# A trunk step on one core: the sample tokens in quarters of the columns, and the first loads and statistics in another order

## What is computed

```
x   = layernorm(x; ln_in)                      # every token over its 1024 columns
h, states = mixer(x)                           # one in-projection, mLSTM and HGRN2 heads, one out-projection
x1  = layernorm(ALPHA * x + h; ln1)
logits = x1 @ w_router + b_router              # 32 experts
top_v, top_i = top_k(logits, 4); gates = softmax(top_v)
y   = sum over the 4 picked experts of gate * expert(x1)   # clamped SwiGLU, 1024 -> 1024 -> 1024
y  += sigmoid(x1 @ w_ple_gate) * (p @ w_ple_proj)
out = layernorm(ALPHA * x1 + y; ln2)
```

## Time and profile before

| | before |
|---|---|
| median of 3 runs | 1262.06 us (1261.76 to 1264.11) |
| the profiled execution, its own time | 1263.85 us |
| its span in the profile | 1262.0 us |
| PE busy | 1166.6 us (92%) |
| DVE busy | 400.7 us (32%) |
| ACT busy | 178.2 us (14%) |
| DMA | 441.92 MB, mean 350 GB/s |

### The profile page before, as it was taken

The page is one execution under the profiler, slowest core; times in us unless marked ns, Lnnn a source line. Parts: engine busy times, 40 slices in busy tenths (PEclk is TensorE's granted clock), DMA queues, the critical chain, the costliest instruction groups (busy, mean ns, idle before and its releaser), DMA issues.

```text
span 1262.0 us, 13214 instructions
## 1 busy us (share of the span) xinstructions
PE 1166.6 (92%) x5599; PEld 483.0 (38%) x5599; DVE 400.7 (32%) x643; ACT 178.2 (14%) x321; POOL 77.2 (6%) x77
## 2 busy tenths in 40 slices
PE   3999999799999997899999999999999999998984
PEld 2777774643333332242333333332323232322221
DVE  6866423841223130112322222232323222214115
ACT  1253242411010110020101010100101010110001
POOL 3100141400101030000000000000000000000000
PEclk9999999899999998999999999999999999999987
DMA  9562111579999999999999999999999999999891
GB/s 313 176 180 67 67 68 67 208 300 420 421 421 421 422 420 386 421 422 421 416 422 421 421 421 421 406 422 420 421 420 421 420 422 412 422 421 413 370 420 55
DMA packets 70029, 441.92 MB, mean 350 GB/s; under 512 B 7824, under 2 KB 7856, under 8 KB 20816
## 3 DMA queue, kind: packets, MB, share of 16 engines
q1 hardware_dynamic: 65168, 425.52, 82.6%
q0 software_dynamic: 4800, 15.51, 3.7%
HBM read 436.28 MB, written 4.73 MB: 349 GB/s over the span
## 4 chain that ended last, share of the span: by engine, by line
PE 70%; DMA 19%; DVE 8%; ACT 2%; issue 1%; SPq 1%; DVEq 0%
PE ps L935 41%; DMA more<-in_w_up 11%; PE ps L543 9%; PE ps L919 5%; PE ps L871 3%; DVE y_s L1740 2%; PE ps L761 2%; DMA ring<-in_w_gate 2%; DMA more<-in_w_down 2%; DMA more<-in_w_gate 2%; PE ps L926 1%; PE ps L571 1%; DVE h_s L1738 1%; ACT hTe L1084 1%; DMA ring<-in_w_up 1%; PE ps L951 1%
## 5 line engine op out<-in xcount | busy, mean ns | idle before, releaser
L935 PE MATMUL ps<-ring,xTe 128*64 128x512 f32 x1536 | 357.4, 602 | 13.4 <-DMA ring<-in_w_up 9.1
L935 PEld LDWEIGHTS ps<-ring,xTe 128*64 128x64 f32 x1536 | 103.9, 136 | 242.0 <-issue 241.8
L1722 DVE TENSOR_TENSOR xs<-xs,ps 128x512 f32<-128x512 f32 (+1 forms) x128 | 70.5, 551 | 365.3 <-PE ps L919 364.7
L935 PE MATMUL ps<-ring,hTe 128*64 128x512 f32 x768 | 181.4, 613 | 4.5 <-DMA ring<-in_w_down 4.5
L935 PE MATMUL ps<-more,xTe 128*64 128x512 f32 x512 | 117.1, 598 | 6.0 <-DMA more<-in_w_up 5.8
L543 PE MATMUL ps<-xT,ring 128*128 128x288 f32 x448 | 116.6, 417 | 1.0 <-PE ps L543 0.6
L935 PEld LDWEIGHTS ps<-ring,hTe 128*64 128x64 f32 x768 | 51.7, 139 | 119.7 <-issue 119.4
L543 PEld LDWEIGHTS ps<-xT,ring 128*128 128x128 f32 x448 | 85.8, 196 | 25.6 <-issue 2.3
L919 PE MATMUL ps<-y_s,GT 128*128 128x512 f32 (+1 forms) x256 | 81.8, 518 | 1.2 <-ACT y_s L1084 1.2
L1738 DVE TENSOR_SCALAR h_s<-ps 128x512 f32<-128x512 f32 x32 | 21.8, 681 | 159.3 <-PE ps L935 159.3
L1754 DVE TENSOR_TENSOR ple<-ple,ps 128x512 f32<-128x512 f32 (+1 forms) x64 | 35.3, 551 | 105.0 <-PE ps L871 90.8
(11 more groups left out here) (344 smaller groups left out, 796.2 us busy)
## 6 DMA issues: line engine op xcount, KB each, us to landing
ring<-in_w_gate SPq DMA_DIRECT2D x96, 1024.0 KB, 10.7
ring<-in_w_up SPq DMA_DIRECT2D x96, 1024.0 KB, 12.1
ring<-in_w_down SPq DMA_DIRECT2D x96, 1024.0 KB, 13.6
more<-in_w_gate SPq DMA_DIRECT2D x32, 1024.0 KB, 12.2
more<-in_w_up SPq DMA_DIRECT2D x32, 1024.0 KB, 12.1
more<-in_w_down SPq DMA_DIRECT2D x32, 1024.0 KB, 13.8
ring<-in_w_in SPq DMA_DIRECT2D x28, 512.0 KB, 6.1
ring<-in_w_out SPq DMA_DIRECT2D x8, 512.0 KB, 5.0
```

Source lines behind the costliest of these rows:

```text
L935: last = mm(ps[64 * q:64 * q + 64, bank0 + half, :], lhs(k, q), wide(t)[:, k % 2, half * 512:(half + 1) * 512], start=False, stop=k == KT - 1)
L1722: last = tt(xs[0:r, i, c], xs[0:r, i, c], new, ALU.add)
```

## The change

1. **Sample tokens in quarters.** The residual of the 32 sample tokens is now `xq`, 128 partitions x 256 columns: partitions 32q to 32q+31 hold columns 256q to 256q+255. Every operation on it is one of 128 x 256 in place of four of 32 x 256 or one of 32 x 1024. Its vectors are `ln_q` (quarters too; eight small loads for each norm). Its statistics need a sum over the four quarters: DVE writes `lnq` (`spread_stats`), PE multiplies it with a matrix of ones and zeros (`row_stats`), and `bn_aggr` reads 24 numbers from PSUM. Two transposes of 128 x 128 in place of eight of 32 x 128 give `xT`; for the router ACT writes each token four times (`xT4`), so that logits and choices lie on all 128 partitions, and the two copies of `row_of` go. The bf16 parts of the samples are made on DVE and ACT in `xbq`, and PE (`sample_rows`) and ACT (`copy_sample_rows`) bring them to `xb_s`. POOL has the subtractions of the prompt tiles only.
2. **The start.** All of x is loaded first, then a quarter of the constants, the vectors, the first four ring slots, the rest of the constants, the other slots. POOL begins its loads when all of x is there. DVE makes the statistics of the three tiles first, then waits for all ten vector loads (L1462 of the new code) and applies the three norms.
3. **Routing stage.** `x1` is now written without a stride; `part` and `rest` of the prompt tiles work with the stride instead. PE routes all three tiles, counts ranks in two steps, and does both `prompt_states` after `sample_ranks`. `OH` is written in halves; the first gather waits for the first half. `neg_v`, a copy for the states and the copy of the counts come after it.
4. **End.** DVE makes the statistics of each tile right after its last share is added. The result of the samples leaves in four loads.

The diff, cut to its core:

```
@@ sync
-            for i, (_, r) in enumerate(TILES):
-                sp.dma_start(xs[0:r, i, :], x_src[i]).then_inc(S[f"x_in{i}"], 16)
-                if i == 0:
-                    sp.dma_start(ln_g[:, :], a["ln_in_g"].partition_broadcast(P)).then_inc(S["ln1_in"], 16)
-                    sp.dma_start(ln_b[:, :], a["ln_in_b"].partition_broadcast(P)).then_inc(S["ln1_in"], 16)
-                    sp.dma_start(cf[:, :], a["const_f"]).then_inc(S["const_in"], 16)
+            for i in range(2):
+                sp.dma_start(xs[:, i, :], x_src[i]).then_inc(S[f"x_in{i}"], 16)
+            for q, x in enumerate(quarters(x_src[2])):
+                sp.dma_start(xq[q * NS:(q + 1) * NS, :], x).then_inc(S["x_in2"], 16)
+            sp.dma_start(cf[:, 0:CF_FIRST], a["const_f"][:, 0:CF_FIRST]).then_inc(S["ident_in"], 16)
+            for n, v in enumerate(("ln_in_g", "ln_in_b")):
+                sp.dma_start((ln_g, ln_b)[n][:, :], a[v].partition_broadcast(P)).then_inc(S["ln1_in"], 16)
+                for q in range(4):
+                    sp.dma_start(ln_q[q * NS:(q + 1) * NS, n, :],
+                                 a[v][q * QW:(q + 1) * QW].partition_broadcast(NS)).then_inc(S["ln1_in"], 16)
...
-            for c0 in W_GROUPS:
+            for n, c0 in enumerate(W_GROUPS):
+                if n == 1:
+                    sp.dma_start(cf[:, CF_FIRST:], a["const_f"][:, CF_FIRST:]).then_inc(S["const_in"], 16)
@@ gpsimd
+            pool.wait_ge(S["x_in2"], 64)
...
-            for i in range(3):
+                out = rests[:, i, :]
+                nc.gpsimd.tensor_tensor(natural(out), natural(out if q else x1[:, i, :]), by_row(xb[:, i, q, :]),
+                                        ALU.subtract).then_inc(S["rest_ok"], 1)
+
+            for i in range(2):
                 for q in range(2):
                     rest(i, q)
@@ tensor
+            def row_stats(n):
+                pe.wait_ge(S["lnq_ok"], n)
+                mm(ps[:, STAT_BANK, 0:24], cf[:, CF_SAME:CF_SAME + P], lnq[:, :, :].rearrange("p q s -> p (q s)"),
+                   start=True, stop=True).then_inc(S["lnq_mm"], 1)
...
-            route(0)
             transpose_normed(1)
+            row_stats(2)
+            route(0)
+            transpose_normed(2)
             route(1)
+            route(2)
+            prompt_ranks()
+            sample_rows()
+            sample_ranks()
             prompt_states_b()
-            transpose_normed(2)
-            route(2)
...
-            pe.wait_ge(S["xT_ok"], 12)
-            prompt_states_a()
-            ranks()
-            pe.wait_ge(S["part_ok"], 9)
-            pe.wait_ge(S["OH_ok"], 1)
+            prompt_states_a()
...
+            pe.wait_ge(S["part_ok"], 8)
+            pe.wait_ge(S["OH_first"], 1)
@@ scalar
+                if i < 2:
+                    f(by_row(xb[:, i, q, :]), natural(rests[:, i, :] if q else x1[:, i, :]), ACT.Copy).then_inc(S["part_ok"], 1)
+                else:
+                    f(xbq[:, q, :], rest_q[:, :] if q else x1q[:, :], ACT.Copy).then_inc(S["partq_ok"], 1)
...
+            part(2, 0)
+            copy_xT(2, 6, 0)
             part(1, 1)
-            part(2, 0)
-            part(1, 2)
-            copy_xT(2, 6, 0)
             part(2, 1)
             part(2, 2)
+            part(1, 2)
+            copy_sample_rows()
@@ vector
+            def spread_stats():
+                tt(lnq[:, :, :], lns[:, 2, 0:1, :].to_broadcast([P, 4, 6]),
+                   cf[:, CF_QUARTER:CF_QUARTER + 4].unsqueeze(2).to_broadcast([P, 4, 6]), ALU.mult).then_inc(S["lnq_ok"], 1)
...
             for i in range(3):
-                dve.wait_ge(S[f"x_in{i}"], 16)
+                dve.wait_ge(S[f"x_in{i}"], 16 if i < 2 else 64)
+                tile_stats(i)
+                if i == 2:
+                    dve.wait_ge(S["ident_in"], 16)
+                    spread_stats()
                 norm_stats(i, i + 1)
-                if i == 0:
-                    dve.wait_ge(S["ln1_in"], 32)
+            dve.wait_ge(S["ln1_in"], 160)
+            for i in range(3):
                 norm_apply(i, i + 1)
...
+            def rest_of_samples(q):
+                dve.wait_ge(S["partq_ok"], q + 1)
+                tt(rest_q[:, :], rest_q[:, :] if q else x1q[:, :], xbq[:, q, :], ALU.subtract).then_inc(S["restq_ok"], 1)
+
+            select(0)
+            rest_of_samples(0)
+            select(1)
+            rest_of_samples(1)
+            select(2)
...
-            for q in (1, 2):
-                step(nc.vector.tensor_copy(row_of[q * NS:(q + 1) * NS, 2, :], row_of[0:NS, 2, :]))
-            step(nc.vector.tensor_copy(ex[:, 3, :], ps[:, 4, P + 3 * NE:P + 4 * NE]))
...
-            add_shares(NPAIR - 1)
+            add_shares(NPAIR - 1, tile_stats)
```

More of the change, by code:

```diff
@@ L103, in trunk_step, with quarters @@
     x_src = [a["x_prompt"][0, 0:P, :], a["x_prompt"][0, P:NP, :], a["x_sample"].rearrange("b t d -> (b t) d")]
+    def quarters(rows):
+        return [rows[:, q * QW:(q + 1) * QW] for q in range(4)]
     p_src = [a["p_prompt"][0, 0, 0:P, :], a["p_prompt"][0, 0, P:NP, :],
@@ L1334, in _, with tile_stats @@
             nc.vector.memset(eps[:, 2:3], 1.0).then_inc(S["setup"], 1)
+            def tile_stats(i, done=None):
+                x = tokens(i)
+                for q in range(2 if i < 2 else 1):
+                    last = nc.vector.bn_stats(lns[:, i, q, :], x[:, q * 512:(q + 1) * 512] if i < 2 else x)
+                    (done or step)(last)
+            def spread_stats():
+                tt(lnq[:, :, :], lns[:, 2, 0:1, :].to_broadcast([P, 4, 6]),
+                   cf[:, CF_QUARTER:CF_QUARTER + 4].unsqueeze(2).to_broadcast([P, 4, 6]), ALU.mult).then_inc(S["lnq_ok"], 1)
@@ L1336, in norm_stats @@
             def norm_stats(i, n):
-                r = TILES[i][1]
-                x = xs[0:r, i, :]
-                for q in range(2):
-                    step(nc.vector.bn_stats(lns[0:r, i, q, :], x[:, q * 512:(q + 1) * 512]))
+                if i == 2:
+                    dve.wait_ge(S["lnq_mm"], n // 3)
                 if n > 3:
                     dve.wait_ge(S["ln_std"], n - 3)
-                nc.vector.bn_aggr(mv[0:r, i, 0:2], lns[0:r, i, :, :].rearrange("p q s -> p (q s)")).then_inc(S["ln_var"], 1)
+                stats = lns[:, i, :, :].rearrange("p q s -> p (q s)") if i < 2 else ps[:, STAT_BANK, 0:24]
@@ L1346, in norm_apply @@
+                nc.vector.bn_aggr(mv[:, i, 0:2], stats).then_inc(S["ln_var"], 1)
             def norm_apply(i, n):
-                r = TILES[i][1]
-                x = xs[0:r, i, :]
+                x = tokens(i)
                 dve.wait_ge(S["ln_var"], n)
-                g, b = (ln_g, ln_b) if n < 7 else (ln2_g, ln2_b)
-                step(stt(x, x, mv[0:r, i, 0:1], g[0:r, :], ALU.subtract, ALU.mult))
-                dve.wait_ge(S["ln_std"], n)
-                step(nc.vector.reciprocal(mv[0:r, i, 3:4], mv[0:r, i, 2:3]))
```

250 lines of the change are left out of this document (155 added, 95 removed).

## The result

| | before | changed |
|---|---|---|
| median | 1261.93 us (4 runs, 1261.76 to 1264.11) | **1276.54 us** (4 runs, 1275.21 to 1277.31) |
| span of the profiled execution | 1262.0 us | 1274.5 us |
| first product of pair 0 | 256.70 | 268.06 |
| last copy of `y_s` | 1239.27 | 1252.85 |
| ACT busy | 178.2 us | 201.4 us |

The ratio (changed over before) is 1.0111, with a 95% interval of 1.0093 to 1.0128: slower by 14.6 us, where 7.7 us less were forecast. The span grew by 12.5 us: start and mixer -2.9 (up to the out-projection's long run of products, at 204.77 in place of 207.68), from there to the first product of pair 0 +14.3, expert stage +2.2, end -1.1. The profile's chain shows what came onto the path: ACT has 4% of it where it had 2, and POOL a first 1%.

What follows compares the result with a forecast made beforehand. The expert stage was taken as DMA-bound and fixed in length, shifting with pair 0's first product. -2.8 (start) - 3.5 (routing) + 0.6 (experts) - 2.0 (end) = -7.7 from the 1262.06 us median gives 1254.3 us; range 1248 to 1260.

Steps and rivals of the forecast that it cites:

- I take 1.0: Routing stage: ACT's and POOL's strided split of the prompt tiles costs 1.0 times the plain one; other bound 1.6.
- The rival: Routing stage: ACT's and POOL's stride delays keys' copies; slower than before from 1.75 times, 1271 us at 2.4; chance 0.05.
- a rival had 1.5: Routing stage: POOL's strided subtractions take 1.5 times, 3.2 us each, pushing the last choice; 1256.4 us, chance 0.2.
- Start: Start: x loaded first lets PE's first projection begin earlier; -2.8 us, bounds -1.5 and -4.8.
- second wait: Start: the projection's seventh and eighth product wait for ring slot 3, limiting 4.8 us earlier to -3.1 us.
- The rest of the routing stage: Routing stage: shorter DVE steps and rank work, less waits for POOL; gather ends 3.5 us earlier, bounds -9 and +2.1.
- The state products: Routing stage: PE does them ahead of the gather; 4.1 us at full clock, 8.0 at half, taken as 6.4.
- DVE steps did end with POOL's operations: Routing stage: a DVE step with two SBUF inputs, or plain SBUF copy, waits for a POOL operation's end.
- the gather: Routing stage: 56 gather products on PE, 4.7 us before, take 3.0 behind busy PE.
- Expert stage: Expert stage: eight more small vector loads, 256 KB at 422 GB/s, +0.6 us, bounds 0 and +1.
- End: End: earlier statistics and a shorter third application, less three more load issues; -2.0 us, bounds -1.2 and -3.
- The branch 0.4: End: the branch between the quarters' statistics and the spread takes 0.4 us.

Runs made afterwards that it cites:

- probe: e2 plus six ACT copies of 128x1024, results unused, varying stride and element size: scattered bf16 writes 4.70 to 5.16 us, fp32 2.01; whole time not given.
- e2: The change, but DVE stores the prompt tiles' x1 with the stride, so ACT's and POOL's prompt work has none: 1261.78 us, ratio 0.9988 to before.
- e5: e2 without the eight small loads of the last norm's quarter vectors, which ACT copies on chip: 1256.84 us, ratio 0.9942 to before.
- e9: The kernel before plus the last norm's eight small loads, into a buffer nothing reads: 1263.84 us, ratio 1.0006 to before.
- e7: e5 plus POOL's spread copies held until OH is built and DVE's register load moved ahead of the last sums: 1256.76 us, ratio 0.9948 to before.
- e1: The change, but ACT and POOL convert in output order, reading with a stride and writing in line: 1261.38 us, ratio 0.9987 to before.

## Why the prediction was wrong

**The step that failed** is in the routing stage: "I take 1.0" for the factor of ACT's and POOL's stride, between bounds of 1.0 and 1.6. ACT's was 4.5. I had taken the nearest row, DVE's store of fp32 (1.6 times), as the upper bound of the unseen operation, and then took the lower. The probe shows why that row was no measure: ACT's strided write of fp32 is 1.9 times, close to DVE's; the element's two bytes make the rest. What was near in kind (a strided store) differed in the one thing that decided. The rival was there with its mechanism, place and condition ("slower from 1.75 times on"), and gives 1271 us at 2.4 times; its chance of 0.05 stood on the same row.

The path of that rival was right. With the measured prices tile 0's chain of parts is 3 x 3.7 us longer on ACT, and 0.7 and 1.5 on POOL: 13.3 us, of which POOL's part is 2.2. It begins 0.7 earlier (DVE's cheaper store), and 2.1 is the wait for PE that ACT had there before. That leaves 10.5, and the keys' copies began 10.1 us late. So the mechanism stood as written, and the price was mis-sized.

**POOL.** 1.35 times where all else was forecast at 1.0 and a rival had 1.5. The Trainium skill, "GPSIMD Engine Reference", on performance pitfalls, has about 50% for reads over 8 bytes apart, in code of one's own on its cores. The trace agrees in kind, with 2.86 us against 2.12.

**Start.** -2.8 forecast, -2.9 measured, by another road, so the agreement is luck. The vectors were there at 12.62, not near 12, and the last norm's transposes and copies brought the projection to 21.82, not 19.6 (2.6 us earlier than before; the mixer gave 0.3 more). The ring slot that was to be the second wait never was one. It landed at 23.0, as forecast, but PE wants it later than I had it: a product is two of the row's records (32 products, x64), so it takes 0.55 us and not 0.28.

**The rest of the routing stage.** With start and a stride factor of 1.0 the first product was to come 6.3 us earlier; in `e2`, where the factor is 1.0 and DVE pays 0.75 us twice instead, it came 4.5 earlier. The state products took 6.1 us (6.4 forecast), DVE steps did end with POOL's operations, and the gather took 3.35 us (3.0).

**Expert stage.** +0.6 forecast from bytes alone, +2.2 measured; 1.7 of it is what these loads cost DMA (`e5`, `e9`). I had priced them by their bytes.

**End.** -2.0 forecast, -1.1 measured. "The branch 0.4" was 1.54 us, of which loading the register was 0.9 (`e7`); the change put it between DVE's statistics and the norms.

The three smaller misses (1.8, 1.6 and 0.9 us) leave 3.4 of the forecast's 7.7 us, which is close to what the spans of `e2` and before differ by (1258.7, 1262.0). By the medians `e2` gains only 0.4 us and `e1` 0.8. The difference is in the executions that were profiled: that of `e2` (1260.46) lay 1.3 us below its kernel's median, and that of before (1263.85) 1.7 above. So the smaller misses, read from one execution of each kernel, are good to a us or two; what makes executions of one kernel differ stays open.

## What to carry to other kernels

When a change moves a conversion of layout to another engine, look at the side that is scattered and at the element's size: here a walk in the order of the output turned 4.76 us into 2.06 with the same bytes, and gave back the whole loss. An operation that no row shows deserves a chance by the spread of its price, above all when it stands ahead of a chain on an in-order engine. In a stage that DMA bounds, don't price small loads by their bytes alone, and take from memory on chip what is already there.
